# ScalarE's order inside an attention step: the exponential of a tile before the copies of the tile turned two steps earlier

## What is computed

```
p = jax.nn.softmax(jnp.concatenate([s_loc, s_ctx, sink], axis=-1), axis=-1)     # mixer A: window, context, sink
p = jax.nn.softmax(s, axis=-1)                                                  # mixer B: all 768 keys
s = jnp.where(valid, s, -jnp.inf)                                               # E and O: a band of 64-token chunks
m = jnp.maximum(jnp.max(s, axis=-1, keepdims=True), sk)                         # E has a sink, O has none
p = jnp.exp(s - m); p = p / (jnp.sum(p, axis=-1, keepdims=True) + jnp.exp(sk - m))
o = jnp.einsum('bhgqj,bjhd->bqhgd', p, v_c)
```

## Time and profile before

| | |
|---|---|
| median of 3 runs | 2383.47 us (2382.32 to 2383.89) |
| the profiled execution | 2386.74 us, its span 2384.9 us |
| granted TensorE clock, mean | 0.947 |
| PE busy | 2200.8 us (92%) |
| DVE, ACT, POOL busy | 1077.2, 843.5, 689.6 us |
| the chain that ended last, by engine | PE 81%, DVE 7%, issue 7%, ACT 2%, POOL 2% |

### The profile page before, as it was taken

How to read it: one execution, slowest core, us unless ns; L and a number is a source line. 1 busy time by engine, 2 the same in 40 slices (tenths; PEclk the granted TensorE clock), 3 DMA queues, 4 the chain that set the end, 5 groups by cost and what they waited for, 6 DMA issues and landing times.

```text
span 2384.9 us, 29805 instructions
## 1 busy us (share of the span) xinstructions
PE 2200.8 (92%) x11468; PEld 1697.5 (71%) x11468; DVE 1077.2 (45%) x1783; ACT 843.5 (35%) x1561; POOL 689.6 (29%) x382
## 2 busy tenths in 40 slices
PE   6899888899999998997998999998998788999996
PEld 5888555587655554885876888886986566788885
DVE  1530788614355533546525625243117724725253
ACT  2321655424354432345123323223116633323222
POOL 1222000252100002430142444444443343444443
PEclk8899999899999999998689999998998989999998
DMA  6221333122100002230012333322231122333331
GB/s 247 66 67 45 89 89 93 49 78 83 36 1 1 1 27 80 72 96 1 27 57 59 106 98 92 103 81 78 90 88 32 32 67 67 98 97 94 101 91 51
DMA packets 255745, 168.63 MB, mean 71 GB/s; under 512 B 5760, under 2 KB 247143, under 8 KB 254455
## 3 DMA queue, kind: packets, MB, share of 16 engines
q1 hardware_dynamic: 251792, 157.31, 22.3%
q0 software_dynamic: 2192, 8.45, 1.1%
q10 hardware_dynamic: 1623, 0.98, 0.1%
HBM read 164.57 MB, written 2.14 MB: 70 GB/s over the span
## 4 chain that ended last, share of the span: by engine, by line
PE 81%; DVE 7%; issue 7%; ACT 2%; POOL 2%; ACTq 0%; DMA 0%; DVEq 0%; POOLq 0%
PE ps L348 18%; PE ps L349 18%; PE ps L350 18%; PE ps L506 8%; PE ps L614 5%; PE ps L578 3%; PE ps L1332 2%; POOL WL L1228 2%; PE ps L978 1%; PE ps L557 1%; DVE MX L519 1%; PE ps L401 1%; PE ps L1529 1%; PE ps L985 1%; PE ps L479 1%
## 5 line engine op out<-in xcount | busy, mean ns | idle before, releaser
L1228 POOL TENSOR_TENSOR WL<-raww,WH 128x1024 fp32r<-128x1024 f32 (+1 forms) x239 | 565.2, 2370 | 992.2 <-ACT WH L303 875.2
L348 PE MATMUL ps<-HH,WH 128*128 128x512 f32 (+1 forms) x1368 | 526.2, 385 | 41.8 <-DVE HL L449 19.6
L349 PE MATMUL ps<-HL,WH 128*128 128x512 f32 (+1 forms) x1368 | 522.2, 382 | 0.0
L350 PE MATMUL ps<-HH,WL 128*128 128x512 f32 (+1 forms) x1368 | 521.6, 381 | 0.0
L303 ACT ACTIVATE WH<-raww 128x1024 fp32r<-128x1024 f32 (+1 forms) x239 | 245.1, 1035 | 328.2 <-PE ps L350 328.1
L348 PEld LDWEIGHTS ps<-HH,WH 128*128 128x128 f32 x1368 | 261.8, 191 | 102.3 <-issue 28.8
L350 PEld LDWEIGHTS ps<-HH,WL 128*128 128x128 f32 x1368 | 261.3, 191 | 49.3
L349 PEld LDWEIGHTS ps<-HL,WH 128*128 128x128 f32 x1368 | 261.7, 191 | 47.1
L531 ACT ACTIVATE PB<-ps,NB 128x256 f32<-128x256 f32 (+5 forms) x256 | 167.9, 656 | 103.9 <-DVE NB L520 65.0
L578 PE MATMUL ps<-ident,PB 128*128 128x128 f32 x952 | 158.3, 283 | 23.3 <-DVE PT L596 16.1
L516 DVE TENSOR_REDUCE NB<-ps 128x1 f32<-128x768 f32 (+4 forms) x128 | 92.5, 723 | 128.4 <-PE ps L506 127.3
(11 more groups left out here) (280 smaller groups left out, 3325.2 us busy)
## 6 DMA issues: line engine op xcount, KB each, us to landing
raww<-in_ffn_w_up SPq DMA_DIRECT2D x88, 512.0 KB, 3.8
raww<-in_ada_w SPq DMA_DIRECT2D x32, 512.0 KB, 3.5
raww<-in_ffn_w_down SPq DMA_DIRECT2D x32, 448.0 KB, 3.7
raww<-in_odd_w_in SPq DMA_DIRECT2D x24, 512.0 KB, 3.7
raww<-in_even_w_in SPq DMA_DIRECT2D x21, 512.0 KB, 3.8
raww<-in_a_w_in SPq DMA_DIRECT2D x20, 512.0 KB, 3.7
raww<-in_ffn_w_down SPq DMA_DIRECT2D x16, 512.0 KB, 3.9
ADA<-in_ada_w SPq DMA_DIRECT2D x6, 1024.0 KB, 10.0
```

The source lines that it names most:

```text
L348: nc.tensor.matmul(out, lh, rh, start=start and k == ks[0], stop=False)
L349: nc.tensor.matmul(out, lh, rl, start=False, stop=False)
L350: ins = nc.tensor.matmul(out, ll, rh, start=False, stop=stop and k == ks[-1])
L1228: nc.gpsimd.tensor_tensor(lo, raw_slot(k), hi.bitcast(F32), ALU.subtract).then_inc(*split_lo.mark(k))
```

## The change

In each step of each attention ACT takes the exponential of tile t first and then the copies of the lots of tile t - 2. Nothing is added or removed.

```diff
         def att_act(act, A):
             for t in range(A["steps"]):
                 r, i = att_at(A, t)
+                if r is not None:
+                    att_exp(act, A, r, i)
                 q, j = att_at(A, t - 2)
                 if q is not None:
                     att_keep("act", A, q, j)
-                if r is not None:
-                    att_exp(act, A, r, i)
                 if t in A["spread_at"]:
                     att_spread_keep(act, A, A["spread_at"][t])
                 if r is not None and "prep_act" in A and r + 1 < len(A["jobs"]):
```

## The result

| | before | after |
|---|---|---|
| median of the runs made side by side | 2382.61 us (2377.97 to 2383.89, 6 runs) | 2394.67 us (2388.87 to 2395.75, 6 runs) |
| the profiled execution | 2386.74 us, span 2384.9 | 2390.58 us, span 2388.8 |
| granted TensorE clock of that execution | 0.947 | 0.949 |
| DVE, ACT, POOL busy in it | 1077.2, 843.5, 689.6 us | 1072.3, 833.2, 692.0 us |

The ratio after to before is 1.0047, with an interval of [1.0033, 1.0061]: the change makes the kernel slower by about 11 us. The forecast was 15.3 us more.

What follows compares the result with a forecast made beforehand. B was taken to run at PE's pace, A near the bound of PE and DVE. Terms 6.8 + 2.0 + 2.6 + 1.7 + 1.9 + 0.3 = 15.3 us on the median 2383.47 gave 2398.8 us, range 2386 to 2410.

Steps and rivals of the forecast that it cites:

- A, products with the values: In A, products with the values wait for a pair's last ACT copy: 2.0 us, between 0 and 6.4.
- I take 0.25 each: In A, delay assumed at each of eight pairs whose latent heads' copy moves back 0.2 to 0.8 us: 2.0 us.
- A, the banks: In A, PE's transposes wait for banks that ACT's later copy empties: 6.8 us, bounds 2.3 and 12.
- 18 x 0.5: In A, about 0.5 us later at 18 places where PE already waits for DVE: 9.0 us before hiding.
- I take three quarters: In A, share of the 9.0 us bank delay that stays, the rest running inside DVE's backlog: 6.8 us.
- A, the clock: In A, added PE waits bring two more falls of the granted clock: 2.6 us, between 0 and 10.4.
- B: In attention B, preparation L978 at seven heads' first tile and the last two steps wait for copies: 1.7 us.
- E and O: Products with the values wait for ACT's copy: E 1.9 us after 0.3 comes back, O 0.3 us for its first pair.
- The tests I had set: Wrong if A grows under 4 us, L531 waits shrink over 5, or time between attentions changes over 2.
- DVE's pace hides it: Rival, chance 0.22: A keeps a quarter of its bank and value terms, no clock fall; 6.7 us slower, 2390.2 us.
- The exponential decides: Rival, chance 0.06: half of PE's 16.1 us waits for exponentials comes back; 8 us faster, 2375.5 us.
- The clock falls in each group: Rival, chance 0.20: eight clock falls in A instead of two, one or two in E and O; 25.1 us slower, 2408.6 us.

Runs made afterwards that it cites:

- second series: The changed kernel run again in the rounds of later experiments, nine runs, against before: 2395.24 us, ratio 1.0043.
- last only: Against before, exponential first only at the steps with ACT's last copy for a pair of heads, all attentions: 2394.13 us, ratio 1.0036.
- after with later products: The whole change, plus products with the values one step later in A's latent pairs, E and O: 2385.98 us, ratio to before 1.0011.
- dose kernels: Two kernels: a_not_last plus one small ACT instruction per changed step, between exponential and copy or behind the copy: 2387.60 and 2382.61 us.
- a_not_last: Against before, exponential first in attention A alone, except at steps with ACT's last copy for a pair: 2382.48 us, ratio 0.9994.
- only in A: Against before, exponential first in attention A alone: 2388.04 us, ratio 1.0020.
- only in E: Against before, exponential first in attention E alone: 2384.43 us, ratio 1.0011.
- dose between: a_not_last plus a small ACT instruction between exponential and copy in each changed step: 2387.60 us, ratio to before 1.0019.
- behind: a_not_last plus the same small ACT instruction after the copy in each changed step: 2382.61 us, ratio to before 1.0002.
- only in B: Against before, exponential first in attention B alone: 2384.03 us, ratio 1.0000.
- only in O: Against before, exponential first in attention O alone: 2386.68 us, ratio 1.0008.

## Why the prediction was right, and where it was not

**Direction and size.** Forecast 15.3 us slower, measured 11.2 by the ratio (7.9 to 14.5), and 10.3 in the second series; 2394.67 us is inside the range. The reason given, a copy queued behind the exponential and its wait for the maximum, is what the traces show: last only and after with later products tie most of the loss to it. That the sum came so near is in part luck: its largest term was 6.8 us too high, the term of the products with the values too low, and the clock took more than it was given.

**A, products with the values: right in kind, too small.** The step that failed is "I take 0.25 each". It had the copy back by 0.2 to 0.8 us and PE waiting in three of eight pairs. In fact PE waits in all eight, 0.4 to 1.9 us each, 7.8 in place of 2.3: 5.5 us more where 2.0 stood, though within the bound of 6.4. In last only, 4.7 us more of this wait made PE's idle time in A 3.3 us longer, so in time the term is nearer to 3 or 4, an estimate from these two numbers. I had priced the move of the copy by its own slack and not by what it is queued behind, which is exponential, sums and sink, 0.65 us, and the wait for the maximum ahead of them. In E I had priced the same chain in full, and the forecast was near.

**A, the banks: the waits came, the loss did not.** "18 x 0.5" was near in number and too high in size: 5.4 us of waits for ACT's copy came at 21 places (14 of L578, 7 of L911), some 0.26 each. Two further steps failed. "I take three quarters" left a quarter to DVE's backlog, and the dose kernels put that share at four tenths. And DVE's and POOL's work was to stay as it was: "L567 moves back by one copy, 0.38 us; POOL, which waits for it, is not near the path". POOL is not, but DVE's L875 beside it is, and it gave 3.1 us back. With 5.4 us less waiting for DVE the term is 0 where 6.8 stood, and a_not_last has its bounds at -4.1 and 1.4.

**A, the clock.** I expected two more falls in A; the profiled executions have three in A before, and two and three in the two of after. The prediction also miscounted the falls of before: its "one such fall in A's steady part" and "seven of eight groups with the same waits have no fall now" leave out a second one, in the last group:

```profile
437.30:440.70 3.40, 3.40 (x15) 2.07 (x14) 1.37 (x3) 1.24 (x4) 0.00 (x0) 0.50 0.02 5
```

Over all runs the mean clock is lower: the six runs of after list granted clocks of 0.945 to 0.949, and their times follow it, 2388.87 and 2390.58 us at 0.949, 2394.4 to 2395.8 at 0.945 and 0.946. The mean is 0.947 over these and 0.946 over the nine of the second series, against 0.949 for the 94 runs of before in the three sets. Among the runs of one kernel, with one slope for all kernels, 0.001 of the clock is worth 1.5 us, so the 0.003 are about 4 us. At equal clock the two series lie 6.1 and 6.4 us above before. So some 4 us of the 11 came with the clock, more than the 2.6 forecast. Where in the program it fell is not shown, only that the profiles have no more falls in A; that the change's small waits bring it about is not shown by any run here. The same measure puts only in A at 3.0 us above before, only in E at 1.8, the dose between at 3.4 and behind at 1.0, and only in B, only in O and a_not_last within 0.4 of before. The recorded clocks have three digits and the runs scatter by about 1 us around the line, so these are estimates.

**B: 1.7 forecast, 1.67 measured** in the trace, at the place that was named, the preparation L978 (1.2 us of waits there, and 0.5 at the last steps).

**E and O.** E's waits for L598 grew by 1.5 us, 1.1 to 2.6, and those of the scores L506 for the exponential shrank from 6.6 to 6.2; 1.9 was forecast, and the timed run, 2.6 us by the ratio, can't tell it from either. In O the waits for L598 grew by 0.7 us and those for the exponential shrank by 0.5; 0.3 was forecast. O is longer by 1.2 us all the same: PE's wait there for DVE's L1098, whose input comes from ACT's preparation, grew from 20.7 to 21.5 us, and the prediction did not look at it.

**The tests I had set.** The waits predicted for A, B and E are there, but A grew by 2.3 us in length and not by 4. The bank term fell away, and after had one fall of the clock less in A; in the second profile of after, with three falls as before has, A is 218.38 us, 2.5 more than before; and the time around the attentions differs by 5.2 us, more than the 2 allowed. That last test was badly chosen: no instruction there moved, and a profiled execution of the same kernel in the second series has 1746.5 us around its attentions, 4.4 more than the first.

**Rivals.** "DVE's pace hides it" asked for 6.7 us in all and was half right: PE's delays do run inside DVE's backlog, by four tenths in the dose kernels, but DVE's own work also became shorter, which it did not foresee, and at the products with the values it asked for 0.5 us where most of the loss was. "The exponential decides" is refuted: PE's waits for L531 shrank by under 1 us in E and O. "The clock falls in each group" didn't come: two or three falls in A, not eight.

What stays open: the four attentions alone add to 9.3 us by their ratios, each with an interval of 3 us either way, so they can't say whether the whole is more than its parts. Open too are why the mean clock is lower with the new order, and how much of what the banks gave back is DVE's shorter work and how much its backlog.

## What to carry to other kernels

When an instruction is moved behind another on an in-order engine, price it by all that it is now queued behind, the wait included, and look first for the consumer that takes its result soonest: here the late last copy of each pair of heads cost most of the 11 us, and starting its consumer a step later left no loss that could be measured. Follow what the move does to bystanders too: a shift of 0.4 us decided which of two engines was slowed by the other, and gave the one that PE waits for 3.1 us back. Do not add waits up as if they were time: with the dose, four tenths of the new waits for ACT came out of old waits for DVE. And where one kernel's runs differ by 10 us, count waits in the trace rather than totals of single profiles.

## What the runs showed of the hardware

- DVE's subtraction of two SBUF tiles and POOL's product slow each other: where they start 0.11 to 0.15 us apart, the one that starts second takes 0.43 us more (1.12 for 0.69 on DVE, 1.16 for 0.73 on POOL), the first nothing. With POOL 0.36 us behind, in the dose kernels, it takes 0.19 more.
- A fall of the granted clock to 0.50, that is 1.2 GHz, for 3.4 us cost B 1.7 us (234.71 to 236.41 with the order of before, 236.38 to 238.05 with the new one): PE is never free there, and the price is half of the fall. The fall at the start of B comes in some executions and kernels and not in others with the same instructions there.
- Runs of one kernel differ by 10 us and more in 2384 (2375.22 to 2389.49 in 32 of before), and most of it follows the mean granted clock: 2375.22 us at 0.954, 2389.49 at 0.945.
